# Two projection units moved by one head in a transformer kernel on one NeuronCore

## The reference

```python
mod = silu(c) @ w_ada + b_ada                 # six shift, scale and gate vectors
h = rmsnorm(x, norm_gains[0]) * (1 + sc1) + sh1
proj = h @ w_in                               # 1024 -> 2304
# 8 heads of full causal attention (qa, ka, va: 512 columns each),
# 8 heads of attention in a window of 128 (qb: 512 columns; kb, vb: 128 each,
# 2 key/value heads, each for 4 query heads; a sink in each softmax);
# every head adds a bias by distance
y = concat(out_a, out_b) @ w_out
x = x + g1 * rmsnorm(y, norm_gains[1])
h = rmsnorm(x, norm_gains[2]) * (1 + sc2) + sh2
x = x + g2 * rmsnorm(square(relu(h @ w1 + b1)) @ w2 + b2, norm_gains[3])
```

## Time and profile before

| | |
|---|---|
| Median of 3 runs | 788.48 us |
| Profiled execution, its own time | 789.94 us |
| Its span, first to last instruction | 788.2 us |
| TensorE busy | 734.8 us, 93% |
| VectorE busy | 517.8 us, 66% |
| ScalarE busy | 450.2 us, 57% |
| Mean granted TensorE clock | 0.974 |

### The profile page before, as it was taken

One profiled execution on the slowest core, in us unless ns is written; L12 is line 12 of the kernel. 1 busy time (PEld: TensorE's weight loads), 2 busy tenths in 40 slices (PEclk: granted clock), 3 DMA queues, 4 the chain that ended last, 5 costly groups with the idle time before them and its releaser, 6 DMA issues.

```text
span 788.2 us, 12072 instructions
## 1 busy us (share of the span) xinstructions
PE 734.8 (93%) x4062; PEld 619.8 (79%) x4062; DVE 517.8 (66%) x764; ACT 450.2 (57%) x724; POOL 44.4 (6%) x77
## 2 busy tenths in 40 slices
PE   0599999789999999989999999999897999999998
PEld 0498966589999886767989777777686888888886
DVE  6877697777877643457657465665747777777443
ACT  1654678666666433355455687554446777777331
POOL 3100100100000100014101000000000000000000
PEclk9899999979999999998999999999997999999999
DMA  8999985257787655534763564544444666656661
GB/s 315 368 330 338 262 278 167 81 150 206 233 240 263 213 187 166 175 117 115 227 189 114 181 187 131 164 125 138 148 123 134 179 188 175 201 175 197 203 196 57
DMA packets 137167, 150.50 MB, mean 191 GB/s; under 512 B 6164, under 2 KB 111783, under 8 KB 137129
## 3 DMA queue, kind: packets, MB, share of 16 engines
q1 hardware_dynamic: 135278, 145.28, 59.9%
q10 hardware_dynamic: 1852, 4.75, 1.7%
HBM read 148.57 MB, written 1.44 MB: 190 GB/s over the span
## 4 chain that ended last, share of the span: by engine, by line
PE 80%; DVE 10%; issue 4%; ACT 3%; DMA 3%; POOL 1%; SPq 0%; POOLq 0%; DVEq 0%; ACTq 0%
PE acc L1363 13%; PE acc L1364 13%; PE acc L1365 13%; PE acc L1355 11%; PE acc L1342 6%; PE acc L1344 6%; PE acc L1343 6%; PE acc L1356 5%; DVE ada_sum L1038 3%; DMA raw<-in_w_ada 2%; PE aux L1331 2%; DVE wl L960 1%; DMA raw<-in_w_out 1%; PE acc L1595 1%; ACT wh L594 1%
## 5 line engine op out<-in xcount | busy, mean ns | idle before, releaser
L960 DVE TENSOR_TENSOR wl<-raw,wh 128x1024 fp32r<-128x1024 f32 x217 | 266.2, 1232 | 149.5 <-ACT wh L594 148.4
L594 ACT ACTIVATE wh<-raw 128x1024 fp32r<-128x1024 f32 x217 | 227.9, 1055 | 125.6 <-PE acc L1365 109.6
L1342 PE MATMUL acc<-xT,wh 128*128 128x256 f32 x440 | 126.9, 288 | 5.5 <-DVE xT L990 4.1
L1355 PE MATMUL acc<-xT,wh 128*128 128x512 f32 x352 | 127.0, 405 | 0.8 <-DVE xT L982 0.8
L1344 PE MATMUL acc<-xT,wl 128*128 128x256 f32 x440 | 126.1, 287 | 0.0
L1343 PE MATMUL acc<-xT,wh 128*128 128x256 f32 x440 | 126.1, 287 | 0.0
L1363 PE MATMUL acc<-wh,xT 128*128 128x512 f32 (+1 forms) x272 | 111.0, 408 | 4.7 <-DVE xT L982 2.6
L1364 PE MATMUL acc<-wl,xT 128*128 128x512 f32 (+1 forms) x272 | 106.5, 391 | 0.0
L1365 PE MATMUL acc<-wh,xT 128*128 128x512 f32 (+1 forms) x272 | 106.3, 391 | 0.0
L1356 PE MATMUL acc<-xT,wl 128*128 128x256 f32 x352 | 100.0, 284 | 0.0
L1342 PEld LDWEIGHTS acc<-xT,wh 128*128 128x128 f32 x440 | 85.9, 195 | 7.5 <-issue 5.9
(11 more groups left out here) (260 smaller groups left out, 877.1 us busy)
## 6 DMA issues: line engine op xcount, KB each, us to landing
raw<-in_w_in SPq DMA_DIRECT2D x66, 512.0 KB, 3.6
raw<-in_w SPq DMA_DIRECT2D x64, 512.0 KB, 3.8
raw<-in_w_ffn_in SPq DMA_DIRECT2D x44, 512.0 KB, 4.1
raw<-in_w_ada SPq DMA_DIRECT2D x27, 512.0 KB, 6.5
raw<-in_w_ffn_out SPq DMA_DIRECT2D x22, 512.0 KB, 4.3
raw_more<-in_w_ada SPq DMA_DIRECT2D x13, 512.0 KB, 7.2
raw<-in_w_out SPq DMA_DIRECT2D x13, 512.0 KB, 4.8
rows_tmp<-in_w_ada ACTq DMA_DIRECT2D x8, 512.0 KB
```

The lines of the kernel that those rows point to most:

```text
L594: A(wh[:, s, :], raw_unit, ACT.Copy).then_inc(rounded, 1)
L960: V.tensor_tensor(wl[:, s, :], raw_slot(r), wh[:, s, :].bitcast(f32), ALU.subtract).then_inc(split_ready, 1)
L1342: mm(bank[:, 0:ROWS], wh[:, s, w], hi, start=(kt == 0), stop=False)
L1355: mm(bank[:, :], wh[:, s, w], moving[:, kt, :], start=(kt == 0), stop=False, skip_group_check=True)
```

## The change

The table `PROJ_SLOTS` gives unit 15 alone to head 2, unit 16 to head 3 and unit 17 to head 4. Units 15 and 16 both ran with head 2, and unit 17 with head 3. TensorE's loop and ScalarE's loop both read the table. `SPLIT_SLOTS` (rounding and low parts), the loads, `OUT_SLOT` and every wait stay as they are.

```diff
-PROJ_SLOTS = {0: [12, 13], 1: [14], 2: [15, 16], 3: [17]}
+PROJ_SLOTS = {0: [12, 13], 1: [14], 2: [15], 3: [16], 4: [17]}
 OUT_SLOT = 5
 SPLIT_SLOTS = {0: [15, 16], 1: [17], 2: [18], 4: [19], 6: [20], 8: [21], 10: [22], 12: [23], 14: [24], 16: [25], 17: [26]}
```

## The result

| | median | runs | span of the profiled execution |
|---|---|---|---|
| before | 789.09 us | 787.53 to 791.08 | 788.2 us |
| after | 800.47 us | 796.52 to 802.73 | 794.8 us |

The changed kernel takes 1.0141 times as long (95% interval 1.0114 to 1.0168): 11.4 us more, where 5.06 us more were forecast. The direction of the forecast holds and its size doesn't; the time lies 3.5 us above the range (790.0 to 797.0).

The account below looks back on a forecast made before the run. The prediction took a transfer to bound the stage up to 91.4 us, VectorE from 95 and TensorE from 125. 2.36 + 1.7 + 1.0 = +5.06 us on the 788.48 us median gave 793.5 us, range 790.0 to 797.0.

Parts of the forecast that it names:

- The idle stretch ahead of unit 17: TensorE idle about 2.8 us ahead of head 2's transposes, until ScalarE's copy of head 1's transposes releases it.
- Term 1: VectorE's split of heads 0 and 1 waits at line 1110 for unit 17: +2.36 us at full clock.
- The rival in which the edit doesn't reach the end: Stall absorbed because a later transfer or wait was late anyway: 788.5 us, chance 0.05.
- the one in which the filler wins: Unit 17 fills the 1.09 us hole ahead of 100.90 and keeps the clock up: 786.15 us, chance 0.07.
- Term 2: Clock drop behind the first new idle stretch, over unit 17: +1.7 us, bounded by 0 and 3.4 us.
- rival 3: Low clock twice as long, 6.6 us behind each gap: 796.2 us, chance 0.10.
- Term 3: Clock drop behind the second idle stretch, over the output projection's first half (1.24 us more) and following steps: +1.0, up to 1.3 us.
- The cover of 0.4 us: At full clock, head 6's scores come at about 110.4 us, before VectorE wants them at 110.78, hiding the late output projection.
- The 0.5 us for the steps behind it: Extra time at low clock for the steps behind the first half of the output projection: about 0.5 us.
- The rule on queues: ScalarE and VectorE work queues strictly in order, so head 4's scores can't pass the waiting split; otherwise 2.36 us becomes near 0.
- The signs of being wrong: VectorE's split starts without a wait, clock stays 1.00 through both gaps, or lag at 125 us isn't that at 103.
- The clock elsewhere: Low-clock stretches in later stages shift against the work: taken as 0, with 1 us either way.

Follow-up runs that it names:

- experiment 10: Changed kernel with ScalarE emptying unit 17's bank ahead of head 4's exponentials: 795.99 us; measured again, 797.65 us beside the changed kernel's 799.04.
- the repeat: The changed kernel itself, unaltered, measured again in the same rounds as a variant that empties unit 17's bank earlier: 799.04 us.
- experiment 4: Changed kernel with eight unused 128 x 512 products right ahead of unit 17 instead of in the first idle stretch: 799.21 us.
- the execution without a drop: Profiled execution, in the second measurement, of the changed kernel with unit 17's bank emptied ahead of head 4's exponentials; clock held behind the 2.67 us gap: 790.49 us.
- experiment 3: Changed kernel with unit 17 as 48 products of 256 columns instead of 128, as long at full clock: 797.19 us.
- experiment 7: Changed kernel with a buffer of its own for the split of heads 0 and 1, so VectorE needn't wait for unit 17: 797.71 us.
- experiment 9: Changed kernel with the rounding and low part of unit 18 in head 3 instead of head 2: 790.36 us.

## Why the forecast was right or wrong

*The idle stretch ahead of unit 17*: right in place, releaser and cause. It was 1.85 us in the profile of the changed kernel and 2.21 in the one beside experiment 10, and 2.8 was forecast. The end of the load of unit 18 moves against TensorE from one execution to the next, and the gap moves with it. ScalarE of the changed kernel at that load:

```profile
91.45 1.06 ACT L594 ACTIVATE wh<-raw 128x1024 fp32r<-128x1024 f32 x1 [4.02 <-DMA raw<-in_w_out]
```

From the first transposes of head 0 to this rounding it is 6.74 us here, 7.10 in the repeat and 7.77 in experiment 4; the gaps are 1.85, 2.21 and 2.89 us, each 4.9 us less. Before it was 7.51 us. The length of the gap doesn't tell whether the clock falls: it fell behind 1.85 us and held behind 2.67.

*Term 1, the stall by order, 2.36 us*: right. It was measured at full clock in three ways: 2.31, 2.33 and 2.34 us (first gap filled, both filled, and the execution without a drop). The stage was 2.40 and 2.50 us longer in the two without any low clock, so nothing absorbed it up to the end of the attention. The rival in which the edit doesn't reach the end falls with that, and so does the one in which the filler wins.

*Term 2, the clock over unit 17, taken at 1.7 with an end at 3.4 us*: this is the step that failed. The stall was 8.19 - 2.31 = 5.9 us longer than at full clock. Of that, unit 17 accounts for 10.29 - 5.41 = 4.9 us, and the transposes, sums and scores ahead of it for 3.04 - 2.07 = 1.0 us (95.21 to 98.25, against 0.42 + 0.80 + 0.85). I had priced the drop by the length of the one low stretch near by, 3.3 us, and the end of the range by twice that, as if a low stretch had a length of its own. In that row the clock rose again over products of 512 columns. The work that the new low stretch would cover was another, 48 products of 128 columns, and no row of before showed those starting at low clock. The fitting bound for a drop was the whole of unit 17 at half speed, 5.4 us more, which together with terms 1 and 3 would have put the upper end near 798 us (about the stage's 9.19 us, and still below the measured 800.47). The argument against rival 3, that unit 17 is dense and long, was wrong by experiments 3, 4 and 7: it is without pauses, and still it didn't bring the clock back.

*Term 3, the second gap, 1.0 us with an end at 1.3*: the gap and its releaser were right. VectorE lost 1.35 us there in the changed kernel and 1.90 + 0.46 = 2.36 us where only the first gap was filled. The cover of 0.4 us is borne out (both gaps filled, the half began at 107.13 and VectorE had no second wait), and so are the 1.24 us of the half itself. The 0.5 us for the steps behind it was too little: transposes, weighted sums and scores took 110.57 to 114.09 = 3.52 us where only the first gap was filled, against 111.56 to 113.63 = 2.07 us for the same steps at full clock before. 1.24 + 1.45 - 0.4 = 2.3 us is the wait of that kernel. In the changed one the clock was back during those steps, at about 116.2.

*The rule on queues*: the trace of after agrees with it. With the split waiting for 8.19 us, the scores of head 4, whose products began at 96.67 and were done by 98.3, weren't touched before it. But the other half of that paragraph, that term 1 would be near 0 if the scores could pass the split, says nothing of the cost at low clock: in experiment 7 they do come first, and VectorE then waits 6.15 us for the next ones.

*The signs of being wrong*: VectorE's split did wait, and the clock did fall. The third, a lag near 125 us that isn't that of 103 us, came true in part. Counted from the first transposes of head 0, VectorE's first split is 7.48 us later than before (24.14 for 16.66) and its second 8.92 us (32.71 for 23.79): the second gap adds 1.4 us. The sum held a term for that gap, so this sign contradicted the forecast's own term 3.

*The clock elsewhere*: the stage makes 9.19 of the 11.4 us, and the interval of the ratio is 9.0 to 13.3 us. The other 2 us or so are in neither profile: what follows the stage takes 640.9 and 643.2 us in the two of the changed kernel, and 644.3 before. Single executions of either kernel differ by more than that (787.5 to 791.1, and 796.5 to 802.7), and where the rest comes from stays open.

*The sum by the runs*, at the stage's end: 2.5 us by order (both gaps filled), 2.4 more with the second drop (+4.92 with the first gap alone filled), 4.3 more with the first (+9.19). Forecast were 2.36, 1.0 and 1.7. These are differences of successive kernels, so they add up to the stage in any case, and the shares depend on their order: in the changed kernel itself VectorE waits 8.19 us at the first split and only 1.35 at the second.

## What to carry to other kernels

Ask of every wait that an edit opens on TensorE what runs directly behind it: the price of a fallen clock is the time of that work at half speed until the clock comes back, not the length of some other low stretch. If that work is narrow products that others wait for, put dense work into the gap; in this kernel 2.0 us of products with no use made it 6 us faster, and the same products behind the drop gained little (stage +9.13 for +9.19). Better still, look for what opens the gap: one load rounded a head later took away 10 us (experiment 9). And where a split or copy waits for the last reader of its buffer, moving that reader moves everything queued behind the split.

## What the runs showed that I had not expected

TensorE ran for 19.50 us without a pause at a granted clock of 0.50 (experiment 7). The Trainium skill ("TensorE: Matmul & The Clock Gate", Part 1) says that the throttled state is the default and that activity releases it. The row shows that an engine which the profile calls busy all the time need not be released; there the measurement decides.

Unit 17's products of 128 columns behave in two ways. Started at 1.00 they kept 1.00 over the whole unit (before, both filled kernels, and the execution without a drop); started at 0.50 they kept 0.50 over the whole unit (changed kernel, only unit 17 moved, own buffer). In all of these it kept to the clock that it started at, also behind the filler of experiment 4, which had brought the clock back.

The same gap was followed by a drop in one execution and not in another of the same kernel (3.04 and 2.67 us idle), whose times run from 790.5 to 800.1 us. A median of a few runs, or a single profile, can hide that; the mean granted clock of every execution doesn't.

The two profiled spans differ by 6.6 us although the attention alone differs by 9.19. Part of it is far off: the up-projection of the second block, which the change doesn't touch, went faster in the profiled execution of after. Line 1355 in both (durations min/median/max in ns, first and last start in us), before and after:

```profile
L1355 PE MATMUL acc<-xT,wh x352: 393/398/766, 598.0 to 724.7; 128*128 128x512 f32 x176
```

```profile
L1355 PE MATMUL acc<-xT,wh x352: 392/395/767, 607.7 to 731.2; 128*128 128x512 f32 x176
```

That is 126.7 us against 123.5 us from the first to the last of the same 352 products. What sets it wasn't looked into; a single span is no measure for a change of this size.
